# Norm factors on the results of four stages instead of on their inputs, and tile-by-tile refills, in a two-layer trunk

## Chip, cores and metric

The kernel runs on one core of a Trainium2 chip. The metric is the device time of one execution in microseconds; the runs are given with their median.

## What is computed

A trunk of two layers over x of 1024 tokens by 1024 features, in float32. Each layer adds a mixer and a gated feed-forward part, each behind an RMS norm:

```python
def rmsnorm(x, g):
    y = xf * lax.rsqrt(jnp.mean(xf * xf, axis=-1, keepdims=True) + RMS_EPS)
    return y * g
...
for l in range(DEPTH):
    h = rmsnorm(x, norm_mix[l])
    proj = h @ w_in[l]
    (u, dq, dk, dv, iq, ik, iw, rq, rk, rv, rg) = jnp.split(proj, split_pts, axis=-1)
    mix = concatenate([s5(u, ...), sparse_attention(dq, dk, dv, iq, ik, iw, ...), retention(rq, rk, rv, rg, ...)])
    x = x + mix @ w_out[l]
    h = rmsnorm(x, norm_ffn[l])
    gate, up = jnp.split(h @ w_ffn_in[l], 2, axis=-1)
    x = x + (silu(gate) * up) @ w_ffn_out[l]
return rmsnorm(x, norm_final)
```

The norm has two parts: a gain for each feature, and a factor 1/rms for each token. Since the matrix product runs over the features, the factor of a token can be multiplied to the product instead of to the input. The sparse attention scores all earlier tokens with a small indexer, keeps the 256 best by 32 rounds of eight maxima each, and attends to those; S5 is a diagonal state-space model; retention is chunkwise.

## The kernel before

**Tiling.** The 1024 tokens are worked on in two halves h of 512. x is kept feature-major: eight tiles of 128 features by 512 tokens (`xs`), the other half waiting in DRAM. The stages are called by layer and half: proj(l,h) with 18 units, mixout(l,h) with 8, ffn(l,h) with 76 (gate and up units that make a chunk of the hidden layer, then down units that add it to x; four chunks of 4, 6, 6 and 6 tiles). A **unit** is one 128-feature tile of results for 512 tokens. The order of stages is proj(0,0), proj(0,1), mixout(0,0), ffn(0,0), mixout(0,1), proj(1,0), ffn(0,1), proj(1,1), mixout(1,0), ffn(1,0), mixout(1,1), ffn(1,1).

**A unit.** A float32 product is made of three passes over halves of the operands: hi x hi, lo x hi and hi x lo, where hi is the operand rounded and lo the rest. A weight tile comes by DMA on SP's queue (three buffers), ACT copies it to `w_hi` (line 723, `prep`, two buffers), POOL subtracts it to `w_lo` (line 625, three buffers). The input tiles stand in `h_hi` and `h_lo`, eight each, for a whole stage: ACT makes hi (`tile_hi`, line 741), POOL the even lo tiles (line 633) and DVE the odd ones (line 1017, 1065). PE (`unit`, line 1511) takes tile by tile hi, lo and the weight's lo, 24 matmuls of 512 columns. In the first unit after a refill (`fresh`) it does all passes on hi tiles first, each behind its `h_hi_ready`, then those on lo tiles. Results alternate between PSUM banks A and B; retention's units of proj go to four banks, token-major.

**The norm between stages.** `norm()` in the plan is three steps, and a fourth fills the tiles. Squares of x are made by ACT after each x tile's last addition (line 737) and added by POOL into `ssq` (line 642). `sums` (line 1619) multiplies ssq by a column of ones into bank F, `rstd` (lines 833 and 1029) makes the factor for each token, with ACT's square root, `spread` (lines 1039 and 1628) turns it into a diagonal on DVE and spreads it over the partitions of bank F by a matmul, and `fillnorm` (line 1044) multiplies each x tile by gain and factor on DVE (line 1061) for ACT and POOL to split. All tiles wait until the last unit of the stage before is done. `fillmix` does the same for the mixers' outputs, with no norm.

**Evictions.** proj: ACT (lines 751 to 771). mixout and down: DVE adds the bank to x (`add_x`, line 1011). Gate: ACT's Silu from the bank (line 796); up: DVE multiplies the bank by it (line 1103), then ACT and POOL split the product to `a_hi` and `a_lo` (lines 801, 696).

**The order of the work.** `plan()` writes one list of steps, and every engine walks it in order and does its share of each step, so an engine's queue is this list. `weave` spreads the side steps of a stage (top-k rounds, scores, attends, retention, S5) among its units by the estimates of `cost`:

```python
    if step[0] == "attend":
        return 0.3 + 2.2 * NK[step[3]] / 1000 * step[5]
...
    def norm():
        return [("sums",), ("rstd", None), ("spread",)]
...
        got += mix[:1] + list(lead) + weave(mix[1:], side[:n_mix], 0, N_OUT - 2) + norm()
        got += [("fillnorm", "xs", DEPTH + l, ffn[0][-1])] + weave(ffn, side[n_mix:], 0, len(ffn) - 10)
```

A stage's list of units has one step more than it has units: the last one, without matmuls, is the eviction of the last unit (the diff calls it the drain).

## Time and profile before

| | us |
|---|---|
| runs, median of 3 | 2931.11 (2929.31 to 2935.93) |
| the profiled execution | 2937.97 |
| its span in the profile | 2936.2 |
| PE busy in the span | 2643.7 (90%) |
| DVE, POOL, ACT busy | 1519.3, 1264.6, 1011.9 |
| mean granted TensorE clock | 0.94 |

The profile is of one execution, so durations are read against its own time, 2937.97. Of the span, 1.8 us lie around the profile. The chain that ended last runs through PE for 72% of the span and through DVE for 16%. "Busy" is summed over an engine's instructions; an engine that is off the chain may idle without cost.

### The profile page before, as it was taken

What the parts mean: (1) busy time and instruction counts of PE and PEld (TensorE: products, weight loads), DVE (VectorE), ACT (ScalarE), POOL (GpSimd) and SP (SyncE); (2) the same over time, 40 slices, a digit from 0 to 9 for tenths busy, and PEclk for the clock granted to TensorE, in tenths of its full rate; (3) what the DMA queues carried; (4) which work ended last, traced back from release to release, by engine and by line L of the source; (5) the groups of instructions that cost most, each with busy time, mean ns of one, the idle gap of its engine ahead of it and who ended that gap; (6) DMA issues with size and microseconds to landing.
All of it is one profiled execution on the core that took longest, in us unless ns stands there. A gap on an engine that the chain in (4) does not pass through costs nothing.

```text
span 2936.2 us, 34071 instructions
## 1 busy us (share of the span) xinstructions
PE 2643.7 (90%) x13418; PEld 2082.3 (71%) x13418; DVE 1519.3 (52%) x2722; ACT 1011.9 (34%) x1492; POOL 1264.6 (43%) x772
## 2 busy tenths in 40 slices
PE   7877687798999998899999989979899989899998
PEld 5666554577777776668877767757677767678887
DVE  4559822669889522663333146566988962211111
ACT  4222133233444443232343532333344344322222
POOL 3322122344444455354544453344444445555555
PEclk9978886999999999999999999999999999999999
DMA  6321110212222125222322242111222222433332
GB/s 154 89 80 47 30 36 1 72 51 72 74 78 79 58 84 148 77 79 72 88 77 82 58 134 64 54 58 51 71 69 83 72 65 79 143 94 99 113 105 93
DMA packets 389735, 230.24 MB, mean 78 GB/s; under 512 B 33576, under 2 KB 376520, under 8 KB 387528
## 3 DMA queue, kind: packets, MB, share of 16 engines
q1 hardware_dynamic: 388256, 225.44, 26.2%
q10 hardware_dynamic: 1320, 2.62, 0.5%
q8 instruction: 107, 1.75, 0.2%
q14 instruction: 52, 0.43, 0.0%
HBM read 211.78 MB, written 14.16 MB: 77 GB/s over the span
## 4 chain that ended last, share of the span: by engine, by line
PE 72%; DVE 16%; ACT 3%; DMA 3%; POOL 3%; issue 2%; SPq 1%; DVEq 0%; POOLq 0%; ACTq 0%
PE psum L1500 69%; DVE scores L1139 3%; DVE top L1137 3%; PE psum L1781 2%; POOL w_lo L625 1%; DVE tmp L1061 1%; DMA w_raw<-in_w_in_dram 1%; DVE xs L1011 1%; DVE scores L1128 1%; DMA w_raw<-in_w_out_dram 1%; DMA x_half<-xs 1%; POOL h_lo L633 1%; ACT scratch L906 1%; ACT w_hi L723 1%; ACT scratch L888 0%
## 5 line engine op out<-in xcount | busy, mean ns | idle before, releaser
L625 POOL TENSOR_TENSOR w_lo<-w_raw,w_hi 128x1024 fp32r<-128x1024 f32 (+2 forms) x408 | 902.5, 2213 | 1396.2 <-ACT w_hi L723 1377.1
L1500 PE MATMUL psum<-h_hi,w_hi 128*128 128x512 f32 x1984 | 814.9, 411 | 57.3 <-POOL w_lo L625 32.7
L1500 PE MATMUL psum<-h_hi,w_lo 128*128 128x512 f32 x1984 | 793.7, 400 | 0.0
L1500 PE MATMUL psum<-h_lo,w_hi 128*128 128x512 f32 x1984 | 771.4, 396 | 0.0
L723 ACT ACTIVATE w_hi<-w_raw 128x1024 fp32r<-128x1024 f32 (+2 forms) x408 | 396.9, 973 | 893.3 <-PE psum L1500 812.9
L1500 PEld LDWEIGHTS psum<-h_hi,w_hi 128*128 128x128 f32 x1984 | 388.3, 196 | 180.7 <-issue 49.8
L1500 PEld LDWEIGHTS psum<-h_hi,w_lo 128*128 128x128 f32 x1984 | 387.0, 195 | 83.0
L1500 PEld LDWEIGHTS psum<-h_lo,w_hi 128*128 128x128 f32 x1984 | 381.0, 192 | 77.1 <-issue 0.5
L1137 DVE MAX8 top<-scores 128x8 f32<-128x512 f32 (+5 forms) x384 | 342.2, 891 | 8.4
L1139 DVE MATCH_REPLACE8 scores<-top,scores 128x512 f32<-128x512 f32 (+5 forms) x384 | 336.3, 876 | 0.0
L1011 DVE TENSOR_TENSOR xs<-xs,psum 128x512 f32<-128x512 f32 x160 | 110.0, 687 | 358.7 <-PE psum L1500 347.7
L1500 PE MATMUL psum<-a_hi,w_hi 128*128 128x512 f32 x704 | 279.9, 398 | 9.1 <-DVE xs L1011 9.1
L1103 DVE TENSOR_TENSOR tmp<-psum,tmp 128x512 f32<-128x512 f32 x88 | 60.8, 691 | 425.7 <-PE psum L1500 413.4
L1500 PE MATMUL psum<-a_lo,w_hi 128*128 128x512 f32 x704 | 276.6, 393 | 0.8 <-POOL a_lo L696 0.8
L1500 PE MATMUL psum<-a_hi,w_lo 128*128 128x512 f32 x704 | 276.3, 393 | 0.0
L1500 PEld LDWEIGHTS psum<-a_hi,w_hi 128*128 128x128 f32 x704 | 133.4, 189 | 43.3 <-POOL w_lo L625 12.4
L1500 PEld LDWEIGHTS psum<-a_lo,w_hi 128*128 128x128 f32 x704 | 133.4, 190 | 30.8 <-POOL a_lo L696 2.5
L796 ACT ACTIVATE tmp<-psum 128x512 f32<-128x512 f32 x88 | 52.6, 598 | 297.2 <-PE psum L1500 297.0
L1500 PEld LDWEIGHTS psum<-a_hi,w_lo 128*128 128x128 f32 x704 | 133.5, 190 | 26.9
L1170 DVE CUSTOM_DVE_ANT_0 psum<-psum,scores 128x384 f32<-128x384 f32 (+5 forms) x48 | 43.1, 899 | 160.9 <-PE psum L1500 160.2
L1500 PE MATMUL psum<-w_hi,h_hi 128*128 128x512 f32 x256 | 106.4, 416 | 16.9 <-POOL w_lo L625 10.0
L696 POOL TENSOR_TENSOR a_lo<-tmp,a_hi 128x512 fp32r<-128x512 f32 x88 | 119.7, 1360 | 0.0
(262 smaller groups left out, 2906.2 us busy)
## 6 DMA issues: line engine op xcount, KB each, us to landing
w_raw<-in_w_ffn_in_dram SPq DMA_DIRECT2D x176, 512.0 KB, 3.8
w_raw<-in_w_ffn_out_dram SPq DMA_DIRECT2D x96, 384.0 KB, 3.4
w_raw<-in_w_in_dram SPq DMA_DIRECT2D x68, 512.0 KB, 3.7
w_raw<-in_w_out_dram SPq DMA_DIRECT2D x32, 512.0 KB, 4.2
w_raw<-in_w_ffn_out_dram SPq DMA_DIRECT2D x32, 256.0 KB, 2.7
x_half<-xs SPq DMA_DIRECT2D x6, 1024.0 KB, 6.1
xs<-x_half SPq DMA_DIRECT2D x6, 1024.0 KB, 7.1
out_dram<-mixed SPq DMA_DIRECT2D x8, 512.0 KB, 3.7
```

The costliest lines, as they stand in the source:

```text
L625: eng.tensor_tensor(w_lo(u, n), w_raw[:, u % 3, 0:n], w_hi[:, u % 2, 0:n].bitcast(F32), ALU.subtract).then_inc(sems["weights_ready"], 1)
L633: eng.tensor_tensor(h_lo[:, k, :], src, h_hi[:, k, :].bitcast(F32), ALU.subtract).then_inc(sems["h_lo_pool"], 1)
L696: eng.tensor_tensor(a_lo[:, f, :], atmp, a_hi[:, f, :].bitcast(F32), ALU.subtract).then_inc(sems["a_lo_ready"], 1)
L723: act(w_hi[:, u % 2, 0:n], w_raw[:, u % 3, 0:n], ACTF.Copy).then_inc(sems["hi_ready"], 1)
L796: act(gate, bank(unit_bank("ffn", i - 1)), ACTF.Silu).then_inc(sems["gate_ready"], 1)
L1011: tt(xs[:, m, :], xs[:, m, :], bank(g), ADD).then_inc(sems["x_added"], 1)
L1103: tt(atmp, bank(g), gate, MUL).then_inc(sems["atmp_ready"], 1)
L1137: eng.max(out=top8[:, :], in_=score[b]).then_inc(sems["round_step"], 1)
L1139: eng.match_replace(out=score[b], in_to_replace=top8[:, :], in_values=score[b], imm_value=TAKEN).then_inc(sems["round_step"], 1)
L1170: eng.tensor_tensor_reduce(bank(g, 0, nk), bank(g, 0, nk), rows_[r], -1.0, 3e38, ADD, ALU.min, nmax[:, i:i + 1]).then_inc(sems["nmax_ready ...
L1500: return eng.matmul(out_, lhsT, rhs, start=start, stop=stop, skip_group_check=True)
L1781: ins = eng.transpose(bank(g, k * P, (k + 1) * P), at_.prob[:, r, k * P:(k + 1) * P], ident)
```

## The change

In four stages, proj(1,1), ffn(0,0), ffn(1,0) and ffn(1,1) (`deferred`), the input tiles are filled with x times gain, without the token's factor, by ACT (`raw_hi`) and DVE (`raw_lo`) alone, each tile once the last unit of the stage before has read it (`tile_read`), or, for proj(1,1), as each x tile is finished. The sums are made inside the first unit, between its hi and lo passes; the last tile's square goes straight into the sums' matmul instead of through POOL's addition, which makes eight one-column products of the four. The factor, spread over the partitions, is copied to an SBUF tile `row` by ACT, and the results are multiplied by it: in proj(1,1) at eviction, now on DVE (`scale_out`), for retention's token-major units as ACT's scale and DVE's scalar; in ffn the gate by DVE (to `scaled`), then Silu on ACT, then a second multiplication by `row` on POOL, which stands for the up result's factor, then the up multiplication as before.

The other refills (proj(0,1), proj(1,0), ffn(0,1), both `fillmix`) also run tile by tile behind `tile_read` (`tile_free`) and stand ahead of the last eviction in the plan; `fillmix` takes the tiles in an order of its own. The plan moves side steps: attends are costed flatter, retention steps 0 to 3 go from proj(0,0) to proj(0,1), the S5 steps of proj(1,1) end by unit 14, and the factor for ffn(0,1) is made after unit 15 of proj(1,0).

The core of the diff ("..." stands for what is left out):

```diff
-        return 0.3 + 2.2 * NK[step[3]] / 1000 * step[5]
+        return 0.3 + (1.7, 2.2)[step[5]] * NK[step[3]] / 1000
...
+    def scales():
+        return [("rstd", None), ("spread", "row")]
...
-    out += weave(main[15:], [("rstd", "boot"), ("spread",)] + blend(retention_steps(0, 0, 0, 4), rounds(2, 20)))
+    out += main[15:16] + [("rstd", "boot"), ("spread", "fill")] + weave(main[16:18], rounds(2, 20))
+    drain = main[18:]
-    out += [("fillnorm", "xa", 0, main[0][-1]), ("dma", "store_x1_first", main[0][-1]), ("dma", "load_bias", 0)]
+    out += [("fillnorm", "xa", 0, main[0][-1], "tmp")] + drain
+    out += [("dma", "store_x1_first", main[0][-1]), ("dma", "load_bias", 0)]
     s5 = [("s5", 0, s) for s in range(14)]
-    out += weave(main[:14], blend(retention_steps(0, 0, 4) + s5, rounds(3)), 2)
+    out += weave(main[:14], blend(retention_steps(0, 0) + s5, rounds(3)), 0)
...
-        got = [] if h else [("fillmix", l, h, mix[0][-1])]
-        got += mix[:1] + list(lead) + weave(mix[1:], side[:n_mix], 0, N_OUT - 2) + norm()
-        got += [("fillnorm", "xs", DEPTH + l, ffn[0][-1])] + weave(ffn, side[n_mix:], 0, len(ffn) - 10)
+        got = mix[:1] + list(lead) + weave(mix[1:N_OUT], side[:n_mix], 0, N_OUT - 2)
+        got += [("fillraw", DEPTH + l, 0)] + mix[N_OUT:] + [("fillraw", DEPTH + l, 1), ("sums", "inside")]
+        got += ffn[:1] + scales() + weave(ffn[1:], side[n_mix:], 0, len(ffn) - 11)
...
-    out += [("fillnorm", "xa", 1, main[0][-1])]
-    side = [("dma", "s5_load1", 0), ("sums",)]
+    out += [("fillnorm", "xa", 1, main[0][-1], "scratch")] + drain
...
-    out += weave(main[7:], sc[:3] + blend(rounds(2), sc[3:]) + [("spread",)])
+    out += weave(main[7:16], sc[:3] + blend(rounds(2), sc[3:])) + [("spread", "fill")] + main[16:18]
     ffn = window("ffn", 0, 1)
-    out += [("fillnorm", "xs", DEPTH, ffn[0][-1])]
+    out += [("fillnorm", "xs", DEPTH, ffn[0][-1], "tmp")] + main[18:]
...
-    out += norm()
     main = window("proj", 1, 1)
-    out += [("fillnorm", "xs", 1, main[0][-1]), ("dma", "swap_x", main[0][-1])]
-    out += weave(main, [("s5", 1, s) for s in range(14)], 2)
+    out += [("sums", "inside")] + main[:1] + scales() + [("dma", "swap_x", main[0][-1])]
+    out += weave(main[1:N_PROJ], [("s5", 1, s) for s in range(14)], 1, 14)
+    out += [("fillmix", 1, 0, counter[0])] + main[N_PROJ:]
...
+def deferred(kind, l, h):
+    return (kind, l, h) == ("proj", 1, 1) or kind == "ffn" and (l, h) != (0, 1)
+def mix_order(l):
+    return (2, 3, 4, 5, 6, 0, 1, 7) if l else (0, 1, 6, 7, 2, 3, 4, 5)
...
-                    eng.wait_ge(sems["norm_tmp"], st.now("norm_tmp"))
+                    eng.wait_ge(sems["h_lo_dve"], st.now("h_lo_dve"))
...
+                        if did == "gate" and deferred(kind, l, h):
+                            eng.wait_ge(sems["gate_ready"], st.add("gate_ready"))
+                            eng.tensor_tensor(gate, gate, row, ALU.mult).then_inc(sems["gate_scaled"], 1)
...
+            def raw_hi(k, gain):
+                act(h_hi[:, k, :], xs[:, k, :], ACTF.Copy, scale=gains[:, gain, k:k + 1]).then_inc(sems["h_hi_ready"], 1)
+            def tile_free(k, u=None):
+                if k < KT - 1:
+                    eng.wait_ge(sems["tile_read"], st.now("tile_read") + k + 1)
+                elif u is not None:
+                    eng.wait_ge(sems["unit_done"], u)
...
+                if did == "gate" and later:
+                    eng.wait_ge(sems["gated"], st.add("gated"))
+                    if st.now("atmp_ready"):
+                        eng.wait_ge(sems["atmp_ready"], st.now("atmp_ready"))
+                    act(gate, scaled, ACTF.Silu).then_inc(sems["gate_ready"], 1)
...
+                        if (l, h) == (0, 1):
+                            eng.wait_ge(sems["x_added"], st.now("x_added"))
+                            raw_hi(f, 1)
...
+                elif what == "fillraw":
+                    for k in (KT - 1,) if step[2] else range(KT - 1):
+                        tile_free(k)
+                        raw_hi(k, step[1])
...
+            def raw_lo(k, gain):
+                eng.wait_ge(sems["h_hi_ready"], st.add("h_hi_ready"))
+                eng.wait_ge(sems["x_added"], st.now("x_added"))
+                stt(h_lo[:, k, :], xs[:, k, :], gains[:, gain, k:k + 1], h_hi[:, k, :].bitcast(F32), MUL, SUB).then_inc(
+                    sems["h_lo_dve"], 1)
+                st.add("h_lo_dve")
...
+            def scale_out(h, j, u):
+                g = unit_bank("proj", j)
+                cols = slice(h * HALF, (h + 1) * HALF)
+                eng.wait_ge(sems["unit_done"], u)
+                eng.wait_ge(sems["row_ready"], st.now("row_ready"))
...
+                else:
+                    ins = tt(iqT[:, j - U_IQ, :] if j < U_RET else qT[:, j - U_Q, :], bank(g), row, MUL)
+                ins.then_inc(sems["proj_out"], 1)
...
+                if did == "gate" and later:
                     eng.wait_ge(sems["unit_done"], u)
-                    eng.wait_ge(sems["gate_ready"], st.add("gate_ready"))
+                    eng.wait_ge(sems["row_ready"], st.now("row_ready"))
+                    if st.now("gate_ready"):
+                        eng.wait_ge(sems["gate_ready"], st.now("gate_ready"))
+                    tt(scaled, bank(g), row, MUL).then_inc(sems["gated"], 1)
...
-            def unit(g, u, sem):
+            def unit(g, u, sem, last=False):
                 hi, lo = w_hi[:, u % 2, :], w_lo(u)
                 eng.wait_ge(sems["weights_ready"], u + 1)
                 take(g)
                 out_ = bank(g)
                 if fresh[0]:
-                    fresh[0] = False
-                    for k in range(KT):
+                    order, low_by = fresh[0]
+                    fresh[0] = None
+                    for n, k in enumerate(order):
                         eng.wait_ge(sems["h_hi_ready"], st.add("h_hi_ready"))
-                        mm(out_, hi[:, k * P:(k + 1) * P], h_hi[:, k, :], k == 0, False)
+                        mm(out_, hi[:, k * P:(k + 1) * P], h_hi[:, k, :], n == 0, False)
                         mm(out_, lo[:, k * P:(k + 1) * P], h_hi[:, k, :], False, False)
-                    for k in range(KT):
-                        by = ("h_lo_pool", "h_lo_dve")[k % 2]
+                    if inside[0]:
+                        inside[0] = False
+                        sums()
+                    for n, k in enumerate(order):
+                        by = low_by[k % 2]
                         eng.wait_ge(sems[by], st.add(by))
-                        ins = mm(out_, hi[:, k * P:(k + 1) * P], h_lo[:, k, :], False, k == KT - 1)
+                        ins = mm(out_, hi[:, k * P:(k + 1) * P], h_lo[:, k, :], False, n == KT - 1)
                 else:
                     for k in range(KT):
                         w = slice(k * P, (k + 1) * P)
                         mm(out_, hi[:, w], h_hi[:, k, :], k == 0, False)
                         mm(out_, hi[:, w], h_lo[:, k, :], False, False)
                         ins = mm(out_, lo[:, w], h_hi[:, k, :], False, k == KT - 1)
+                        if last and k < KT - 1:
+                            ins.then_inc(sems["tile_read"], 1)
...
-                eng.wait_ge(sems["ssq_added"], st.add("ssq_added", KT - 1))
+                eng.wait_ge(sems["ssq_added"], st.add("ssq_added", KT - 2))
+                eng.wait_ge(sems["square_ready"], st.add("square_ready", KT))
                 take("F")
                 for t in range(TT):
-                    ins = mm(bank("F", t, t + 1), ssq[:, t * P:(t + 1) * P], ones[:, 0:1], True, True)
+                    mm(bank("F", t, t + 1), ssq[:, t * P:(t + 1) * P], ones[:, 0:1], True, False)
+                    ins = mm(bank("F", t, t + 1), atmp[:, t * P:(t + 1) * P], ones[:, 0:1], False, True)
                 ins.then_inc(sems["sums_ready"], 1)
                 leave("F", "mean_ready")
-            def spread():
+            def spread(what):
                 eng.wait_ge(sems["diag_ready"], st.add("diag_ready"))
                 take("F")
-                mm(bank("F"), ones, gate, True, True).then_inc(sems["spread_ready"], 1)
-                leave("F", "norm_tmp", KT)
+                mm(bank("F"), ones, scaled, True, True).then_inc(sems["spread_ready"], 1)
+                if what == "row":
+                    leave("F", "row_ready")
+                else:
+                    leave("F", "norm_tmp", KT)
```

## Rows read from the trace of the kernel before

**Rows 1.** The page's busy time of each engine: us, share of the span, instructions.

```profile
PE 2643.7 (90%) x13418; PEld 2082.3 (71%) x13418; DVE 1519.3 (52%) x2722; ACT 1011.9 (34%) x1492; POOL 1264.6 (43%) x772
```

**Rows 2.** Timeline, two following units of proj(0,1): start us, us, engine line op, out<-in.

```profile
182.75 0.39 PE L1500 MATMUL psum<-h_hi,w_hi 128*128 128x512 f32 x1
...
188.19 0.39 PE L1500 MATMUL psum<-h_hi,w_hi 128*128 128x512 f32 x1
```

**Rows 3.** Timeline, end of ffn(0,1) to proj(1,1); in brackets idle before and releaser.

```profile
1729.85 0.39 PE L1500 MATMUL psum<-a_lo,w_hi 128*128 128x512 f32 x1
...
1731.70 1.26 POOL L642 TENSOR_TENSOR ssq<-ssq,tmp 128x512 f32<-128x512 f32 x1 [0.74 <-ACT tmp L737]
...
1733.02 1.05 PE L1500 MATMUL psum<-cst,ssq 128*128 128x1 f32 x8 [2.78 <-POOL ssq L642]
...
1735.50 2.08 PE L1500 MATMUL psum<-tmp,cst 128*128 128x512 f32 x2 [1.43 <-DVE tmp L1041]
...
1748.82 0.50 PE L1500 MATMUL psum<-h_hi,w_hi 128*128 128x512 f32 x1 [1.31 <-POOL w_lo L625]
```

**Rows 4.** Timeline, TensorE, mixout(0,0)'s last matmul and ffn(0,0)'s second unit.

```profile
579.61 0.39 PE L1500 MATMUL psum<-h_hi,w_lo 128*128 128x512 f32 x1
...
601.23 0.51 PE L1500 MATMUL psum<-h_hi,w_hi 128*128 128x512 f32 x1
```

**Rows 5.** VectorE's lines L1103 and L1391 (ns min/median/max); timeline of the first S5 step.

```profile
L1103 DVE TENSOR_TENSOR tmp<-psum,tmp x88: 681/692/692, 607.5 to 2889.1; 128x512 f32<-128x512 f32 x88
...
L1391 DVE TENSOR_TENSOR scratch<-s5p,s_bb x8: 691/693/2851, 248.8 to 1819.8; 128x512 f32<-128x512 f32 x8
...
1746.46 2.85 DVE L1391 TENSOR_TENSOR scratch<-s5p,s_bb 128x512 f32<-128x512 f32 x1
...
1757.81 0.69 DVE L1397 TENSOR_TENSOR area<-scratch 64x512 f32<-64x512 f32 x1
```

**Rows 6.** Timeline, TensorE, the factor's matmul in mixout(0,1).

```profile
1133.94 1.02 PE L1500 MATMUL psum<-tmp,cst 128*128 128x512 f32 x2
```

**Rows 7.** Gate eviction (page: busy, mean ns, idle) and POOL's low halves (ns min/median/max).

```profile
L796 ACT ACTIVATE tmp<-psum 128x512 f32<-128x512 f32 x88 | 52.6, 598 | 297.2 <-PE psum L1500 297.0
...
L625 POOL TENSOR_TENSOR w_lo<-w_raw,w_hi x408: 1263/2388/3450, 19.6 to 2915.1; 128x1024 fp32r<-128x1024 f32 x96, 128x768 fp32r<-128x768 f32 x28, 128x512 fp32r<-128x512 f32 x12
```

**Rows 8.** Stretches: us, busy of PE, PEld, DVE, ACT, POOL (x), PEclk, DMA share, GB/s.

```profile
176.00:200.00 24.00, 22.67 (x110) 18.51 (x109) 4.96 (x13) 3.54 (x6) 7.67 (x4) 0.93 0.25 67
260.00:300.00 40.00, 35.14 (x268) 27.98 (x266) 38.46 (x96) 7.50 (x10) 7.26 (x3) 0.93 0.14 40
702.00:776.00 74.00, 74.00 (x389) 59.79 (x390) 62.11 (x102) 34.54 (x50) 36.67 (x23) 0.98 0.25 72
776.00:828.00 52.00, 48.87 (x261) 38.35 (x261) 50.33 (x74) 17.10 (x25) 23.68 (x18) 1.00 0.26 74
```

**Rows 9.** Timeline, end of proj(0,0) to the norm for proj(0,1).

```profile
142.90 1.21 DVE L1196 TENSOR_TENSOR scratch<-scratch,cst 128x1024 f32<-128x1024 f32 x1
...
155.22 0.39 PE L1500 MATMUL psum<-h_hi,w_lo 128*128 128x512 f32 x1
...
167.76 2.71 DVE L1061 SCALAR_TENSOR_TENSOR tmp<-area,gains,psum 128x512 f32<-128x512 f32 x4
```

**Rows 10.** Timeline, TensorE: proj(1,0) to ffn(0,1), then the S5 output to mixout(1,0).

```profile
1277.17 0.39 PE L1500 MATMUL psum<-h_hi,w_lo 128*128 128x512 f32 x1
...
1294.51 0.50 PE L1500 MATMUL psum<-h_hi,w_hi 128*128 128x512 f32 x1 [1.30 <-POOL w_lo L625]
...
1890.05 7.03 PE L1500 MATMUL psum<-uy,s_glu 128*128 128x512 f32 x16
...
1910.73 0.50 PE L1500 MATMUL psum<-h_hi,w_hi 128*128 128x512 f32 x1 [1.28 <-POOL w_lo L625]
```

**Rows 11.** Timeline, TensorE, one attend step of block 7 in ffn(0,0).

```profile
1006.84 2.75 PE L1781 MATMUL psum<-cst,scratch 128*128 128x128 f32 x16 [2.62 <-ACT scratch L906]
```

**Rows 12.** The page's group of the top-k rounds' first operation (busy, mean ns, idle).

```profile
L1137 DVE MAX8 top<-scores 128x8 f32<-128x512 f32 (+5 forms) x384 | 342.2, 891 | 8.4
```

More of the change, by code:

```diff
@@ L353, in part @@
             return where[:, first:first + n].rearrange(pattern, **sizes)
-        gate, atmp = tmp[:, 2, :], tmp[:, 3, :]
+        row, scaled, gate, atmp = (tmp[:, i, :] for i in range(4))
         xa = area[:, 0:4096].rearrange("p (k c) -> p k c", k=KT)
@@ L584, in _ @@
                         [383, P], [P * 384, HEADS], [1, 256]])).then_inc(sems["bias_loaded"], 16)
-                elif what == "fillnorm":
-                    st.add("norm_tmp", KT)
+                elif what in ("fillnorm", "fillmix"):
+                    st.add("h_lo_dve", KT // 2)
+                elif what == "fillraw" and step[2]:
+                    st.add("h_lo_dve", KT)
                 elif step[:2] == ("dma", "store_x1_first"):
@@ L791, in ffn @@
                 did, c, f = FFN[i - 1] if i else (None, 0, 0)
-                if did == "gate":
+                later = deferred("ffn", l, h)
+                if did == "gate" and not later:
                     eng.wait_ge(sems["unit_done"], u)
@@ L1874, in _ @@
                 elif what == "sums":
-                    sums()
+                    if step[1] == "inside":
+                        inside[0] = True
+                    else:
+                        sums()
                 elif what == "rstd":
```

171 lines of the change are left out of this document (125 added, 46 removed).

## The prediction

> **What bounds the kernel now.** I began with the busy time of each engine over the span: TensorE (PE) is busy 90% of it, VectorE (DVE) 52%, GpSimd (POOL) 43%, ScalarE (ACT) 34% [rows 1]. So a gain must come from PE's idle 10%, or from work that PE itself needn't do. Next I read the timeline at the ends of the stages, since there each engine works for the next and PE can only wait. The measure is a unit: inside a stage, the first matmuls of two following units stand 5.44 us apart [rows 2], which is 24 matmuls of 0.227. Where a stage hands over, I take the end of its last unit (start of the last matmul plus 0.23) and the start of the second unit of the next stage; what that distance has above 5.44 is lost.
>
> Between ffn(0,1) and proj(1,1) the last matmul starts at 1729.85 and the second unit at 1748.82 [rows 3]: 18.74 us, **13.3 lost**. The rows between show why: POOL's last addition of squares (1.26), the sums on PE (1.05), 1.43 until the factor's matmul, then that matmul (2.08), and only then are the eight input tiles normed, copied and split. mixout(1,1) to ffn(1,1) repeats it to 0.1. mixout(0,0) to ffn(0,0) has 601.23 - 579.84 = 21.4 [rows 4]; without the unit and eight score matmuls (8 x 0.227 = 1.8) it is 14.1, and mixout(1,0) to ffn(1,0) repeats it. The four add up to 54.8.
>
> **The change, part by part**
>
> *Norm factors on the results, four stages.* The tiles need no factor now, so ACT and DVE refill each as the last unit leaves it. Tile 7 comes last: addition 0.69 (a DVE operation of this size [rows 5]), then a square and a copy on ACT; PE's 16 hi matmuls of the first unit take 3.6 us, so the tile is there before its turn. What stays on PE's path is the sums, doubled (the last square now enters by matmuls of its own, 2 x 1.05 = 2.1), and the factor's matmul, 1.02 where the clock is up [rows 6], against 2.08 in the junction now. The factor needs 1.43 after the sums and eight lo matmuls (1.8) cover that. The second unit's weights (ACT copy, then POOL 2.39 [rows 7]) are ready near 5.7 us after the junction's start, PE needs them at 7.5. So about 3.1 stays at each of four junctions, 12.4 in all: **+42.4**. With the factor's matmul at its low-clock price it would be 38.2.
>
> *The gate's new path.* In 66 gates of three ffn stages the eviction was one ACT operation (0.60 [rows 7]) and is now DVE 0.69, ACT 0.60, POOL 1.26 (the size of POOL's addition [rows 3]), then DVE as before. PE waits for none of it directly: the bank is free after the first. POOL does the next weights first (ACT copy about 1, POOL 2.39, to 3.4 after the unit's end) and its multiplication ends near 5.0, before the up unit ends at 5.44, when DVE needs it. I take **0**. The cover is the idle of these engines: in a stretch of ffn(0,0) with about two top-k rounds to a unit DVE is busy 62.11 of 74 us and POOL 36.67 [rows 8], and per pair of units (10.9 us) the change adds 0.69 and 1.26. Where DVE has no idle (776 to 828: 50.33 of 52 [rows 8]) mostly downs run, which have no gate.
>
> A DVE operation with two inputs in SBUF took 2.85 us instead of 0.69 while POOL worked [rows 5], and the up multiplication, which reads one input from PSUM, took 0.68 to 0.69 in all 88 cases [rows 5]. The Trainium skill, "SBUF — State Buffer", section "SBUF: two separate sides", says that a VectorE operation with two SBUF inputs and a GpSimd operation that reads SBUF hold one port pair in turn, each for its whole length; this speaks against the change, since its new POOL multiplications read SBUF. By that rule every one could hold DVE up to 1.26 us; by the rows half or more of the eight such operations weren't held at all (median 0.69 [rows 5]). My sum goes by the rows, and the other price is in the first rival.
>
> *proj(0,0) to proj(0,1).* Last unit's end 155.45, then eight DVE operations of the retention kind (one of 1.21 has its row) run ahead of the norm's DVE work, which starts at 167.76 [rows 9]. The change moves these retention steps into proj(0,1), so 8 x 1.21 = 9.7 us leave the path. There they meet DVE idle 19 of 24 us at the stage's start, but DVE busy 38.46 of 40 later on [rows 8]. Bounds: 0, if the later stretch pays it all back, and 19, if that idle takes all that was waited for. I take the nearest row: **+10**.
>
> *The other refills.* proj(1,0) to ffn(0,1): 1294.51 - 1277.40 = 17.1 [rows 10], 11.7 lost. The factor is now ready before the last unit ends and the tiles are filled while it runs; the matmul for the factor (1.02) and about 1 of DVE wait stay: **+9.5**. mixout(0,1) to proj(1,0) gets the same treatment, but ACT's last square and the second unit's weights stand behind the refill, bounds 0 and 9.5; I take **+1**, since its factor is on the chip well before the end already (its matmul is the one of [rows 6]), so only the refill itself gets earlier. mixout(1,0)'s inputs: PE ends the S5 output at 1897.08 (1890.05 + 7.03) and the second unit starts at 1910.73 [rows 10], 8.2 lost; filling five tiles ahead of the S5 tiles hides it: **+8**. The same in layer 0, where the attention's tiles come last and are only there when the attention is: bounds 0 and 8.2, near the low one, **+1.5**.
>
> *Side steps.* In proj(1,1) the S5 steps are squeezed from units 2 to 18 into 2 to 14, and all evictions move from ACT to DVE, behind them. The first S5 step holds DVE from 1746.46 to 1758.5, 12.0 us [rows 5]; one unit of cover leaves 6.6: **-7** (without the slow operations it is about 4.3 shorter, so -2; twice, -13). The last attends of ffn(0,0) and ffn(1,0) now come nearly one to a unit. Back to back, PE waits 2.62 before one [rows 11], some 3 with the step after it; two such pairs less per stage, two stages: **+12** (0 if the waits only move). In exchange the downs of chunk 2 get 16 rounds instead of 14: two rounds of two operations of 0.89 [rows 12] are 3.6 us on a DVE without idle, **-6** for two stages with a little taken off. The DMAs that swap x in proj(1,1) stand one unit later on SP's queue and wait for the eight low tiles; weight loads queue behind them, but run up to three units ahead (16 us), and that wait ends by the first unit's end: 0.
>
> *Sums elsewhere.* Three more sums double (3 x 1.05): **-3**. At the very end POOL's 1.26 goes and 1.05 comes: **+0.2**.
>
> **Sum:** 42.4 + 10 + 9.5 + 1 + 8 + 1.5 - 7 + 12 - 6 - 3 + 0.2 = 68.6. The profiled execution took 2937.97 us (span 2936.2); so it would take 2869.4. The median of the runs is 6.9 below that execution, so the prediction is **2862**. The three runs lie 0.23% apart, so 0.2% (6 us) is about what can be told from no change.
>
> **Rivals**
>
> *VectorE gives part back.* The proj(0,1) gain is eaten by the stage's own DVE-bound stretch (-10), S5 stalls PE twice (-6 more), the attends' waits only move (-12), and POOL's multiplications hold DVE as in the 2.85 case [rows 5]: the 74 us [rows 8] hold seven pairs, 7 x (0.69 + 1.26) = 13.7 against 11.9 us of idle, 1.8 over, and some three such stretches lie in the two stages (-6, rounded up). This leaves 34.6: **2896**. For it: DVE 38.46 of 40 [rows 8]. Against: the first three items need a stretch without idle, and DVE has idle in most. By the rule of the Trainium skill ("SBUF — State Buffer", as above) the last item is the likely one.
>
> *More comes free.* proj(0,1) takes its full 19 (+9), S5 costs only 2 (+5), the extra rounds lie in idle (+6): **2842**.
>
> *The gate's path becomes the bound, and the kernel slower.* POOL works in order: if DVE takes up a gate's result late, because a round or an S5 or attend piece is ahead of it, ACT's Silu and POOL's multiplication wait, and behind that POOL's next weights wait, for which PE waits. It decides once the multiplication ends over 3 us later than 5.0. At 2 us in each of 44 gates with side work, 88 us: 2950. At 1.5 to 1.7 it only cancels the gain. For it: three engines in a row instead of one; against: 3 us of slack, and DVE's free time [rows 8].
>
> *Deferring does nothing.* If tile 7, or the sums inside the first unit, hold the second unit as long as the normed fill does now, 42.4 go: 2905. The junction's rows speak against it [rows 3], as nearly all of the 13.3 lies in steps that the tiles don't need any more.
>
> **How the numbers follow.** Forecast 0.62 (own range 2850 to 2875), VectorE gives back 0.15, more free 0.10, deferral without effect 0.03, gate path 0.10 (0.07 slower, 0.03 no change). The range 2838 to 2896 holds the first three, with a little more at the low end for the low-end terms together. Faster 0.90, same 0.03, slower 0.07.
>
> **What would show it.** Right: at the four junctions the second unit starts some 8.5 us after the last unit's end (10.4 with the scores); the factor's matmul after the first unit takes about 1; a gate's POOL multiplication ends before its up unit; PE's wait for POOL's weights doesn't grow in ffn(0,0). Wrong in part: PE idle before DVE operations early in proj(1,1), or proj(0,1) as long as before by its end. Wrong altogether: PE idle before w_lo in most gates, with POOL waiting for ACT's Silu.

## The result and the profile after

The changed kernel took **2907.41 us** (median of 4 runs, 2898.05 to 2907.97) against 2932.86 before (median of 4 runs); the ratio is 0.9903, 95% interval 0.989 to 0.9916. It is faster by 1.0%. Forecast were 2862 us and 2838 to 2896, so the sign is right, and the gain is 25 us of the 69 that were summed up.

The page of the changed kernel, the busy time of its engines [rows 1] and the shares of the chain that ended last:

```profile
span 2905.5 us, 34447 instructions
PE 2638.2 (91%) x13482; PEld 2082.5 (72%) x13482; DVE 1558.2 (54%) x2784; ACT 1013.9 (35%) x1484; POOL 1313.1 (45%) x814
...
PE 70%; DVE 18%; issue 3%; ACT 3%; POOL 3%; DMA 2%; SPq 0%; DVEq 0%; ACTq 0%; POOLq 0%
```

PE is busy 5.5 us less, although it has 64 more one-column matmuls to do; the share of the chain that ended last on VectorE rose from 16% to 18%. To see where the time went I cut the execution at the ends of the stages (start of a stage's last matmul plus 0.23) and set the lengths beside the forecast's terms (us):

| from the end of the stage before to the end of | before | after | gain | forecast |
|---|---|---|---|---|
| proj(0,0) | 155.5 | 155.5 | 0.0 | 0 |
| proj(0,1) | 280.3 | 280.2 | 0.1 | 10 |
| mixout(0,0) | 144.1 | 140.9 | 3.2 | 1.5 |
| ffn(0,0) | 516.9 | 512.1 | 4.8 | 14 |
| mixout(0,1), proj(1,0), ffn(0,1) | 633.4 | 634.0 | -0.7 | 8.4 |
| proj(1,1), mixout(1,0) | 246.6 | 237.7 | 9.0 | 11.2 |
| ffn(1,0) | 515.6 | 510.6 | 5.1 | 14 |
| mixout(1,1), ffn(1,1), the end | 443.8 | 434.6 | 9.3 | 9.4 |

The sum is 30.7, the difference of the two profiled spans. (14 is deferring 11, attends 6, rounds -3; the 11.2 and 9.4 are sums of the prediction's terms in the same way.) Three places miss: proj(0,1) by 10, the group with proj(1,0) by 9, ffn(0,0) and ffn(1,0) by 9 each. The rest is within 2.2, though two of the rows agree only as sums: proj(1,1) grew by 2.5 and mixout(1,0) shrank by 11.5 (forecast were 3.2 and 8 less), since S5 steps that ran behind proj(1,1) now run in it.

The junctions themselves came out nearly as forecast. Timeline of PE at the end of ffn(0,1) [rows 3] (the columns are those of [rows 2]):

```profile
1722.48 0.39 PE L1638 MATMUL psum<-a_lo,w_hi 128*128 128x512 f32 x1
1722.70 0.39 PE L1638 MATMUL psum<-h_hi,w_hi 128*128 128x512 f32 x1
...
1726.33 0.28 PE L1638 MATMUL psum<-cst,ssq 128*128 128x1 f32 x2
...
1728.03 2.11 PE L1638 MATMUL psum<-h_lo,w_hi 128*128 128x512 f32 x8
1729.98 1.02 PE L1638 MATMUL psum<-tmp,cst 128*128 128x512 f32 x2
1730.44 0.79 PE L1638 MATMUL psum<-h_hi,w_hi 128*128 128x512 f32 x1
```

The first unit follows the last without a gap, the sums take 1.70 (to 1728.03), the factor 0.46, and the second unit starts 7.73 after the end of the stage: 2.3 lost where it was 13.3, and 3.1 forecast. At ffn(0,0) the same 7.73. But two units on in ffn(0,0) [rows 4]:

```profile
576.56 0.39 PE L1638 MATMUL psum<-h_hi,w_hi 128*128 128x512 f32 x1
...
584.29 0.79 PE L1638 MATMUL psum<-h_hi,w_hi 128*128 128x512 f32 x1
...
592.08 1.99 PE L1638 MATMUL psum<-ikT,iqT 64*128 64x512 f32 x8 [1.74 <-DVE scores L1257]
...
605.54 2.82 PE L1959 MATMUL psum<-cst,scratch 128*128 128x128 f32 x12 [5.79 <-DVE scratch L1332]
```

PE waits 1.74 us for the score step's VectorE operation and 5.79 for the retention step's. Before, the scores' wait (2.0) lay in the time that the junction lost anyway, and PE waited 0.33 for the retention's operation. In all, PE's waits from the end of mixout(0,0) to the end of unit 20 of ffn(0,0) (counted from 0) come to 16.5 us before and 16.4 after: the junction's time became waits for the side steps.

proj(0,1) shows the swap most plainly. The matmul that stood behind the normed fill [rows 9] waited 11.67 in the kernel before:

```profile
174.41 0.79 PE L1500 MATMUL psum<-mixed 64*128 64x128 f32 x2 [11.67 <-DVE tmp L1061]
```

and in the kernel after the tiles cost 4.18, and the next wait is 11.74 for the retention steps that were moved here:

```profile
158.20 2.72 DVE L1151 SCALAR_TENSOR_TENSOR tmp<-area,gains,psum 128x512 f32<-128x512 f32 x4
...
159.81 0.77 PE L1638 MATMUL psum<-h_hi,w_hi 128*128 128x512 f32 x1 [4.18 <-ACT h_hi L777]
...
167.05 6.70 POOL L646 TENSOR_TENSOR w_lo<-w_raw,w_hi 128x1024 fp32r<-128x1024 f32 x2 [0.48 <-ACT w_hi L753]
...
168.18 3.36 DVE L1326 TENSOR_TENSOR scratch<-scratch,cst 128x1024 f32<-128x1024 f32 x1
...
179.93 1.33 PE L1959 MATMUL psum<-cst,scratch 128*128 128x128 f32 x5 [11.74 <-DVE scratch L1332]
...
1157.13 0.50 PE L1638 MATMUL psum<-h_hi,w_hi 128*128 128x512 f32 x1 [3.64 <-POOL w_lo L646]
...
1209.72 1.50 PE L1638 MATMUL psum<-ikT,iqT 64*128 64x384 f32 x4 [2.03 <-DVE scores L1257]
1213.19 2.08 PE L1638 MATMUL psum<-ikT,iqT 64*128 64x512 f32 x4 [1.97 <-DVE scores L1257]
...
1265.64 1.12 PE L1638 MATMUL psum<-tmp,cst 128*128 128x512 f32 x2 [1.39 <-DVE tmp L1123]
```

The fill does start 9.6 us earlier (158.20 against 167.76), as the forecast's 9.7 has it. But the moved steps now stand behind it on VectorE, up to 179.9, and one of their operations took 3.36 us instead of 1.21, while POOL made the weights' low halves. The last four lines are of proj(1,0): the second unit waits 3.64 for its weights (1.32 before), PE waits twice about 2.0 for scores (once before), and 1.39 for the factor's diagonal in the middle of the stage.

### The profile page after: what moved, and what is told of

It is laid out like the page before. It is cut to its first block, busy times and chain, and to the rows that moved or that the text cites. A ratio compares the mean times of both kernels' runs of the same rounds, so it can differ in the third digit from the quotient of the medians.

```text
span 2905.5 us, 34447 instructions
## 1 busy us (share of the span) xinstructions
PE 2638.2 (91%) x13482; PEld 2082.5 (72%) x13482; DVE 1558.2 (54%) x2784; ACT 1013.9 (35%) x1484; POOL 1313.1 (45%) x814
## 4 chain that ended last, share of the span: by engine, by line
PE 70%; DVE 18%; issue 3%; ACT 3%; POOL 3%; DMA 2%; SPq 0%; DVEq 0%; ACTq 0%; POOLq 0%
PE psum L1638 66%; DVE scores L1268 4%; DVE top L1266 4%; PE psum L1933 2%; POOL w_lo L646 2%; DMA w_raw<-in_w_in_dram 1%; DVE scores L1257 1%; DVE xs L1093 1%; DMA w_raw<-in_w_out_dram 1%; ACT scratch L971 1%; ACT w_hi L753 1%; POOL h_lo L654 1%; DVE psum L1299 0%; PE psum L1819 0%; DMA x_half<-xs 0%
## 5 line engine op out<-in xcount | busy, mean ns | idle before, releaser
L1230 DVE TENSOR_TENSOR tmp<-psum,tmp 128x512 f32<-128x512 f32 x88 | 60.8, 691 | 280.7 <-PE psum L1638 279.5
L1219 DVE TENSOR_TENSOR tmp<-psum,tmp 128x512 f32<-128x512 f32 x66 | 45.5, 690 | 130.0 <-PE psum L1638 121.5
```

Source lines behind the costliest of these rows:

```text
L1219: tt(scaled, bank(g), row, MUL).then_inc(sems["gated"], 1)
L1230: tt(atmp, bank(g), gate, MUL).then_inc(sems["atmp_ready"], 1)
```

## The experiments

Of each run the stage lengths below are taken as in the table above, from its profile; a stage that no edit touches still scatters from run to run: proj(0,0) from 153.5 to 157.2, proj(0,1) of the changed kernel from 277.1 to 280.3, proj(1,0) from 132.6 to 136.0, ffn(0,1) from 440.4 to 445.2 and ffn(1,1) from 368.7 to 370.4, but ffn(0,0) only from 511.6 to 512.2 and ffn(1,0) from 510.6 to 512.3. The scatter goes with TensorE's mean granted clock: proj(1,0) took 136.0 at 0.92 and 132.6 at 0.96, ffn(0,1) 445.2 at 0.98 and 440.4 at 0.99, and the changed kernel's four runs 2907 to 2908 at 0.945 to 0.947 and 2898.05 at 0.950. So medians less than about 10 us apart say little by themselves; the stages that an edit touches say more.

### Is it VectorE's throughput? Half of the rounds, in both kernels

```diff
-    return [("round", b, r) for r in range(first, last)]
+    return [("round", b, r) for r in range(first, last) if r % 2]
```

> The kernel before with every second top-k round left out in all blocks (16 of 32, so that another set of tokens is attended to), in the same places of the plan. It is the base for the next run and tells little alone. If VectorE's rounds set the pace of proj(0,1), proj(1,0) and the ffn stages of half 0, it is 60 us or more faster than the kernel before; if PE sets it, within 20 us.

> The changed kernel with the same rounds left out. Theory (VectorE's work sets the length of the stages in which the junctions' gain was lost): without half of the rounds the gain stays, so ffn(0,0) and ffn(1,0), from the end of the stage before to their own end, are 11 us or more shorter than in the base run (they were 4.8 and 5.1 shorter with all rounds), proj(1,0) is no more than 2 us longer (was 7.5 longer), and the pair lies 45 us or more apart (was 31). Rival (the gates' longer path costs PE something in each gate, whatever the rounds): ffn(0,0) and ffn(1,0) stay about 5 shorter and the pair about 31 apart.

Measured: 2860.3 and 2820.65 us, 39.7 apart (47.1 in the profiled spans), between the two expectations. proj(1,0) was only 2.4 longer (7.5 with all rounds). ffn(0,0) became 8.2 shorter, ffn(1,0) 4.1, proj(0,1) 1.1. So the theory holds nearly for proj(1,0) (2.4 for 2), half for ffn(0,0) (8.2 for 11), and fails for ffn(1,0) and proj(0,1): with half of the rounds gone the junction's time is lost there all the same. The amount of VectorE's work carries a part of the loss (the pair lies 14 us further apart than with all rounds), not all of it. The plan places side steps by their cost, so with fewer rounds they also stand in other units; the pair doesn't separate the two.

### Is it the gate's longer path?

```diff
-                    eng.wait_ge(sems["gated"], st.add("gated"))
+                    eng.wait_ge(sems["unit_done"], u)
...
-                    act(gate, scaled, ACTF.Silu).then_inc(sems["gate_ready"], 1)
+                    act(gate, bank(unit_bank("ffn", i - 1)), ACTF.Silu).then_inc(sems["gate_ready"], 1)
...
```

> The changed kernel with the gates evicted as before, by ACT's Silu straight from PSUM; the token factor inside Silu is left out, POOL's multiplication stays. Theory: VectorE gets 22 x 0.69 us back in each of the deferred ffn stages; where it sets the pace (about the first 13 units of ffn(0,0) and ffn(1,0)) this shortens the stage: 5 to 9 us less in each of the two, within 1.5 us in ffn(1,1), in all 10 to 18 us less than the changed kernel. Rival (the loss is from the side steps standing one unit later, or from POOL): under 3 us each.

```diff
-                            eng.tensor_tensor(gate, gate, row, ALU.mult).then_inc(sems["gate_scaled"], 1)
```

> The changed kernel without POOL's multiplication of the gate by the factor (the up result's factor is left out). Theory (VectorE's own work is what counts): within 2 us in ffn(0,0), ffn(1,0) and ffn(1,1) each. Rival (POOL's multiplication holds VectorE at the SBUF port or delays POOL's weights): 4 to 13 us less in ffn(0,0) and ffn(1,0) each, and VectorE's max and match-replace operations are shorter in the mean there.

Measured: 2899.09 and 2900.97 us. With plain gates ffn(0,0) was 2.5 shorter, ffn(1,0) 0.7 longer, ffn(1,1) 1.8 shorter; without POOL's multiplication 0.0, 1.7 longer and 1.8 shorter. The medians are 8.3 and 6.4 below the changed kernel's, but of the profiled spans' 7.9 and 5.2 only 3.6 and 0.1 lie in the three stages that the edits touch; the rest is scatter elsewhere, and so is the 1.8 in ffn(1,1) (368.7 in runs that leave it as it is). The first run's theory (5 to 9 us from each of two stages) falls, with 2.5 from one; of the second run the theory stands and the rival falls: neither the 66 VectorE operations nor POOL's hold up much. Taking the gate's path at 0 was right within 4 us. By line, the changed kernel's operations (ns min/median/max):

```profile
L1219 DVE TENSOR_TENSOR tmp<-psum,tmp x66: 677/692/693, 585.6 to 2851.8; 128x512 f32<-128x512 f32 x66
...
L717 POOL TENSOR_TENSOR tmp<-tmp x66: 1268/1294/1491, 588.9 to 2854.5; 128x512 f32<-128x512 f32 x66
```

### Do the side steps stand in the wrong place?

With the gate's path gone and the rounds explaining only a part, what was left was where the plan puts the side steps. First the units of before, behind the scales:

```diff
-        return 0.3 + (1.7, 2.2)[step[5]] * NK[step[3]] / 1000
+        return 0.3 + 2.2 * NK[step[3]] / 1000 * step[5]
...
-        got += ffn[:1] + scales() + weave(ffn[1:], side[n_mix:], 0, len(ffn) - 11)
+        woven = weave(ffn, side[n_mix:], 0, len(ffn) - 10)
+        got += woven[:1] + scales() + woven[1:]
```

> The changed kernel with the side steps of ffn(0,0) and ffn(1,0) in the units in which they stood before (from unit 0 on, behind the scales, and with the old cost of attends). New theory, since gates and rounds explained too little: the junction's gain is lost where the plan now lets PE run into a retention step (PE waited 5.8 us for its VectorE operation in unit 2, 3.3 in unit 13), as the side steps start one unit later and are woven tighter. Then that wait goes from 5.8 to under 2 and the two ffn stages are 4 to 8 us shorter each, less what the attends of block 7 lose again (2 to 4). Rival (VectorE's total work sets the pace, wherever the steps stand): the wait shows up elsewhere, and each stage is within 2 us of the changed kernel.

Measured (run side_old): 2916.34 us, ffn(0,0) 4.5 and ffn(1,0) 8.1 longer than in the changed kernel. PE's waits in ffn(0,0):

```profile
588.80 3.42 PE L1639 MATMUL psum<-ikT,iqT 64*128 64x512 f32 x8 [4.33 <-DVE scores L1258]
...
604.83 1.97 PE L1960 MATMUL psum<-cst,scratch 128*128 128x128 f32 x16 [1.50 <-DVE scratch L1333]
...
671.59 0.47 PE L1639 MATMUL psum<-a_hi,w_hi 128*128 128x512 f32 x1 [3.02 <-DVE xs L1094]
678.59 0.76 PE L1639 MATMUL psum<-a_hi,w_hi 128*128 128x512 f32 x1 [3.99 <-DVE xs L1094]
...
697.90 0.80 PE L1639 MATMUL psum<-h_hi,w_hi 128*128 128x512 f32 x1 [2.52 <-POOL w_lo L647]
```

The 5.79 is 1.50 now, but the scores' wait is 4.33 instead of 1.74, and the later ones are longer too: up to unit 20 PE's waits for VectorE and POOL come to 15.9 with the old places and 15.7 with the new. The rival is right here as far as the wait goes: it moves. On the stages' lengths it is wrong (it said within 2), and so is the theory, which had them shorter. The length comes mostly from the attends: their old cost is dearer at the end of the side work: units 57 to 66 take 3.7 us longer in ffn(0,0) and 7.2 in ffn(1,0), so the flatter attends bring about the 6 per stage that they were given.

Then further apart instead of earlier:

```diff
+    if step[0] in ("scores", "retention") and step[2] == 1 and step[3] >= (7 if step[0] == "scores" else 2):
+        return 4.5
```

> The changed kernel with the last score steps and the retention steps of ffn(0,0) and ffn(1,0) set further apart (their estimate in the plan 4.5 instead of 2 and 3), so that a unit more lies between two of them; the attends of block 7 get denser for it (3, 3 and 2 to a unit). Theory: after the faster junction PE stands at the next link of a chain (scores: PE, ACT, VectorE; retention: VectorE, PE) before the link ahead is done, and what the junction gave is waited away there; with a unit between, PE's waits for retention's VectorE operations (5.8 and 3.3 us) and scores (1.7) fall to under 4 in all, 5 us or more less up to the end of unit 16, of which the attends take back 2 to 5. Rival (the sum of the work on VectorE sets the pace there): the waits for VectorE up to unit 20 stay above 9 us in all.

Measured (run space): 2917.57 us. The waits for scores and retention up to unit 20 fell from 10.8 to 5.2 (5.79 to 1.51, the other retention wait 3.27 to 1.94), but ffn(0,0) is 10.3 longer, ffn(1,0) 5.9: PE's waits for ACT in the denser attends after unit 20 rose from 12.6 to 23.3. Apart, the links do seem to cover each other, nearly as the theory says (5.2 for under 4); but the edit also moves seven of 34 top-k rounds and two of three attends out of the first 20 units, so less is asked of VectorE there, and that work has to be done later: it costs more at the other end.

### What deferring is worth in ffn(0,0) and ffn(1,0)

```diff
-    return (kind, l, h) == ("proj", 1, 1) or kind == "ffn" and (l, h) != (0, 1)
+    return (kind, l, h) == ("proj", 1, 1) or kind == "ffn" and (l, h) == (1, 1)
...
+        if h == 0:
+            got = mix[:1] + list(lead) + weave(mix[1:], side[:n_mix], 0, N_OUT - 2)
+            got += [("sums", None), ("rstd", None), ("spread", "fill"), ("fillnorm", "xs", DEPTH + l, ffn[0][-1], "tmp")]
+            return got + ffn[:1] + weave(ffn[1:], side[n_mix:], 0, len(ffn) - 11)
```

> The changed kernel with the normed fill back in ffn(0,0) and ffn(1,0) (sums, factor and fill between the stages, plain gates), all side steps where the change puts them. Theory: of the 13.3 us that deferring takes out of the junction, little is left at the stage's end, so these two stages are no more than 6 us longer each than in the changed kernel, and PE's waits for scores and retention in units 1 to 3 fall, since the junction covers them. Rival (as I predicted: the junction's time comes straight off the end, and something else in the stage costs it): 10 us or more longer each.

Measured (run norm_ffn0): 2914.27 us; ffn(0,0) is 6.7 longer than in the changed kernel and ffn(1,0) 5.3, one just above the theory's 6 and one below. The second unit ends 10.3 us later. By unit 20 the lead of the deferred fill is 9.6 in ffn(0,0) and 11.2 in ffn(1,0); then it melts, 1.8 where the downs with many rounds begin (unit 30), 1.0 in two places after that, 3.0 at block 7's attends in ffn(1,0) alone. One thing speaks against the theory: the retention wait is the same with the normed fill.

```profile
580.48 2.08 PE L1642 MATMUL psum<-tmp,cst 128*128 128x512 f32 x2 [1.43 <-DVE tmp L1127]
...
593.80 0.50 PE L1642 MATMUL psum<-h_hi,w_hi 128*128 128x512 f32 x1 [1.23 <-POOL w_lo L650]
...
612.92 1.33 PE L1963 MATMUL psum<-cst,scratch 128*128 128x128 f32 x5 [5.82 <-DVE scratch L1336]
```

So that wait belongs to the new places of the steps, not to the faster junction. The four kernels side by side, from the end of mixout(0,0) to the end of unit 20 of ffn(0,0):

| us | side steps of before | side steps of the change |
|---|---|---|
| normed fill | 149.1 (before) | 157.5 (norm_ffn0) |
| deferred | 148.9 (side_old) | 147.8 (the change) |

The new places have one top-k round more done by then. With the old places the first unit ends 10.0 us earlier (7.3 instead of 17.3 after the stage before), and by unit 20 **0.2** of it is left; with the new places deferring gives 9.6, but the new places alone cost 8.3. Together 1.3 is left by unit 20.

The whole stages, ffn(0,0) and ffn(1,0), tell it differently:

| us | side steps of before | side steps of the change |
|---|---|---|
| normed fill | 516.9, 515.6 | 518.8, 515.9 |
| deferred | 516.6, 518.7 | 512.1, 510.6 |

Most of the 8.3 comes back at the attends of units 57 to 66, which are 6 us shorter with the new places. By the end the new places alone cost 1.9 and about 0.2, and deferring alone gives 0.3 and loses 3.1; only the two together gain, 4.8 and 5.1.

### proj(0,1): one wait for another

```diff
-    out += main[15:16] + [("rstd", "boot"), ("spread", "fill")] + weave(main[16:18], rounds(2, 20))
+    out += main[15:16] + [("rstd", "boot"), ("spread", "fill"), ("retention", 0, 0, 0)]
+    out += weave(main[16:18], blend(retention_steps(0, 0, 1, 3), rounds(2, 20)))
...
+    out += [("retention", 0, 0, 3)]
...
-    out += weave(main[:14], blend(retention_steps(0, 0) + s5, rounds(3)), 0)
+    out += weave(main[:14], blend(retention_steps(0, 0, 4) + s5, rounds(3)), 2)
```

> The changed kernel with retention steps 0 to 3 back in proj(0,0). Theory: in proj(0,1) one wait took the place of another (PE waited 11.7 us for the normed tiles before, now 11.7 for the retention's VectorE operation), because both stand in VectorE's queue one behind the other. Then with the steps back PE waits again about 8 to 12 us for the tiles, the 11.7 at the retention falls to under 3, and the stage is as long as now within 4 us. Rival (the tile-by-tile refill alone brings the gain, and the moved steps cost it): the stage is 8 us or more shorter.

```diff
-    out += weave(main[:14], blend(retention_steps(0, 0) + s5, rounds(3)), 0)
+    out += weave(main[:6], blend(retention_steps(0, 0), rounds(3, 0, 12)), 2)
+    out += weave(main[6:14], blend(s5, rounds(3, 12)))
```

> The changed kernel with all 14 retention steps of proj(0,1) in units 2 to 5 instead of 0 to 5, and S5 from unit 6. Theory as in the run before: what lacks is cover on PE while VectorE works off the refill and the first retention steps, so with three units ahead of them (16 us) the 11.7 us wait falls to under 3 and the stage is 5 us or more shorter. Rival (the chain of retention and S5 steps between VectorE, ACT and PE sets the stage's length): the wait moves to later steps, and the stage is within 4 us of now.

Measured (runs ret_back and ret_from2): 2908.93 us with the steps back, the stage 283.9 (280.2 in the changed kernel). The waits are again at the early retention steps, 4.18 and then 13.69 ahead of the matmul that waited 11.67 before:

```profile
159.95 3.68 PE L1961 MATMUL psum<-cst,scratch 128*128 128x128 f32 x16 [4.18 <-DVE scratch L1334]
...
176.19 1.03 ACT L993 ACTIVATE mixed<-psum 128x1024 f32<-128x1024 f32 x1
...
177.31 1.24 PE L1640 MATMUL psum<-mixed 64*128 64x128 f32 x8 [13.69 <-issue]
```

The profile names no releaser for the 13.69, but ACT's copy to `mixed` ends at 177.22, just before that matmul; it stands behind the refill's copies on ACT. So the theory holds in the main: moving steps across the boundary moves the wait. The edit is not quite the old order: step 3 stands behind the refill here, ahead of it in the kernel before. mixout(0,0), too, took 144.8 in that run, near the 144.1 of the kernel before, against 140.9 in the changed kernel, at a granted clock of 0.76 against 0.81. Over both stages the moved steps are thus worth 7.6; with the refill but without them the two stages are 4.3 longer than in the kernel before. How much of that is the clock is not shown. With more units ahead of them (ret_from2, 2901.22 us) the 11.74 falls to 0.47, but the stage is 277.0, no shorter than the unchanged one of norm_ffn0 (277.1): later waits, at retention's end (12.42) and between S5 steps, take it. The second theory falls to its rival, as the wait moves on. That the chain of links between PE, ACT and VectorE alone sets the length of proj(0,1) is not shown: with half of the rounds the stage is 17 to 18 us shorter in either kernel (263.5 and 262.4), so VectorE's load counts there as well.

### proj(1,0): rounds squeezed ahead of the factor

```diff
-    out += weave(main[7:16], sc[:3] + blend(rounds(2), sc[3:])) + [("spread", "fill")] + main[16:18]
+    woven = weave(main[7:18], sc[:3] + blend(rounds(2, 0, 24), sc[3:]))
+    at = woven.index(main[16])
+    out += woven[:at] + [("spread", "fill")] + woven[at:]
...
-    side = blend(retention_steps(1, 0), rounds(3, 0, 16)) + attend_steps(1, 0, 0)
+    side = rounds(2, 24) + blend(retention_steps(1, 0), rounds(3, 0, 16)) + attend_steps(1, 0, 0)
```

> The changed kernel with the top-k rounds of block 2 spread over units 7 to 17 of proj(1,0), the last eight of 32 in the first units of ffn(0,1), and the factor's matmul still after unit 15. Theory: proj(1,0) grew by 7.5 us as 32 rounds and the score steps were squeezed into nine units (PE's waits for scores rose from 2.0 to 5.1, and it waited 1.4 for the factor's diagonal); relaxed, proj(1,0) is 3 to 5 us shorter and ffn(0,1) no more than 1 longer. Rival (the growth is from the doubled sums and from the second unit's weights, 3.6 us at w_lo): under 2 shorter.

Measured (run proj10_later): **2891.73 us**, ratio to the kernel before 0.9862 (0.9846 to 0.9879), against 0.9903 (0.989 to 0.9916) of the change. proj(1,0) is 126.5, 7.2 shorter than in the changed kernel, which is more than the theory said, and ffn(0,1), at 440.3, took over the last eight rounds for nothing (it has 440.4 untouched in two other runs). The untouched proj(1,0) scatters from 132.6 to 136.0; at the same granted clock of 0.96 it is 132.6, so 6.1 of the 7.2 don't come from the clock. Of the 20 us between the two profiled executions the other 13 lie in stages that the edit leaves alone, or in ffn(0,1), which is as short in runs without it. The two extra waits are gone; what is left of the three in the changed kernel is one for scores, beside the second unit's weights:

```profile
1155.84 0.50 PE L1640 MATMUL psum<-h_hi,w_hi 128*128 128x512 f32 x1 [3.62 <-POOL w_lo L648]
...
1209.12 0.92 PE L1640 MATMUL psum<-ikT,iqT 64*128 64x384 f32 x4 [2.03 <-DVE scores L1259]
```

### Together

> The changed kernel with the rounds of block 2 spread as in proj10_later and the retention steps of proj(0,1) as in ret_from2. If the two gains are of different stages, they add up: proj(0,1) about 277, proj(1,0) and ffn(0,1) together 12 us less than the changed kernel, the median 2885 to 2890. If they were partly chance from run to run, the median is nearer to 2900.

The second adds to this:

```diff
-    out += [("fillnorm", "xa", 1, main[0][-1], "scratch")] + drain
+    out += [("fillnorm", "xa", 1, main[0][-1], "scratch")] + main[:1] + drain
```

> As combo1, and at the start of proj(1,0) ACT copies the second unit's weights ahead of the last square. Theory: the refill gains little there since the second unit then waits 3.6 us for its weights, which stand behind the refill and the square on ACT; with the square behind them this wait falls by 1 to 2 us. Rival (POOL's own low tiles hold them): no change within 0.5.

Measured (runs combo1 and combo2): 2891.47 and 2890.24 us (0.9867 and 0.9863, with intervals that hold both and proj10_later). The expected 2885 to 2890 was just missed: proj(1,0) and ffn(0,1) together are 8.9 and 14.2 shorter than in the changed kernel, around the 12 expected, but ret_from2's edit adds nothing: proj(0,1) was 277.5 and 279.9 in these two. The weights' wait did fall:

```profile
1154.00 0.50 PE L1641 MATMUL psum<-h_hi,w_hi 128*128 128x512 f32 x1 [1.30 <-POOL w_lo L649]
```

It was 3.66 in combo1 and is 1.30 here, a little more than the theory's 1 to 2 less, and proj(1,0) is 122.9 instead of 127.2 (at a granted clock of 0.97 instead of 0.95). The medians of all three lie about 16 us below the changed kernel's; 7.2, 6.5 and 10.8 of that are seen in proj(1,0), the rest is not tied to an edit.

## Why the prediction was wrong

**Right.** The junctions: forecast 3.1 left at each, measured 2.3 at three and 5.0 at ffn(1,1), where PE waits 1.1 for the last tile, which the forecast had there in time, and the granted clock is 0.77 from that wait to the second unit. The gain up to the second units is 54.8 - 11.9 = 42.9, forecast 42.4; that it agrees so closely is partly luck, as the deviations cancel. It stayed where no side chain follows: mixout(1,1) to the end gained 9.3 of 9.4 (in parts 2.6, 7.8 and -1.2). The gate's path at 0: right within 4 us, shown by two runs. The refill of mixout(1,0): with proj(1,1) 9.0 of 11.2. The attends: 3.7 and 7.2, forecast 6. mixout(0,0) gained 3.2 where 1.5 was forecast for its refill, but it gained nothing in ret_back, which has that refill; so this gain is not shown to be the refill's.

**Wrong step 1: a junction's time counted as the stage's.** "42.4" was taken whole from the end of the kernel. In ffn(0,0) and ffn(1,0) the side steps follow at once, as a chain (PE's scores, ACT, VectorE, PE's retention, VectorE), and before the change part of that chain ran while PE stood at the junction. I saw the score matmuls there and took out only their 1.8 us of work, not the wait in front of them. The tables of four kernels show the rest: deferring alone gives 0.2 by unit 20 of ffn(0,0), and at the stages' ends 0.3 and -3.1; with the new places of the side steps it gives 6.7 and 5.3, where 11 was forecast. Which link sets the pace in the first 20 units is still open: half of the rounds and plain gates did not free it.

**Wrong step 2: the moved side steps of ffn(0,0) and ffn(1,0) counted by their attends alone.** That they start a unit later and are woven tighter stands in the diff, and I priced only block 7 and chunk 2. With the normed fill their new places cost 8.3 us up to unit 20; the attends later return 6 of that, and at the stages' ends 1.9 and 0.2 are lost, where a gain of 3 each was forecast (6 for the attends less 3 for the rounds).

**Wrong step 3: proj(0,1), +10.** I bounded it with 0 at the low end, and VectorE's idle 19 of 24 us at the stage's start made me take the "nearest row". But that idle was time in which VectorE had nothing to do yet, not room: PE needs the moved steps' results at once, and waited 11.74 for them. Measured 0.1; the first rival had this item, though as a loss in the later stretch.

**Wrong step 4: proj(1,0) to ffn(0,1), +9.5, with "about 1 of DVE wait".** The refill brought most of what it should (the second unit of ffn(0,1) starts 9.55 after the end of proj(1,0), 17.1 before, 7.6 gained of 9.5). But to have the factor ready, 32 rounds and the scores were squeezed into nine units. That cost proj(1,0) 7.5 us, and proj10_later gives back 7.2.

**The rivals.** "VectorE gives part back" was the right one by kind, at 2896; its item for proj(0,1) held in direction, its second S5 stall did not come (PE waits 5.60 once for the first S5 step of proj(1,1), where the forecast itself had 6.6), the attends' waits did not only move, its item on POOL's multiplications did not happen (without them ffn(0,0) is as long and ffn(1,0) no shorter), and it had neither ffn(0,0)'s first units nor proj(1,0). By the rule of the Trainium skill ("SBUF — State Buffer", "SBUF: two separate sides") the 66 new POOL operations could hold VectorE; no run here shows that these cost time. POOL's making of the weights' low halves, which the kernel before has too, did hold one in proj(0,1): the 3.36 us above lie in the chain that PE waited for. "The gate's path becomes the bound" and "deferring does nothing" are refuted as they were put. The second has the nearest number, 2905, but by luck: the second units do start 7.73 us after the stage's end, and the gain is spent behind them. The range was too narrow because all that it held shared the junction's 42.4.

## What to carry to other kernels

A gap on the busiest engine is worth its length only if nothing that follows was being made ready in it: before counting it, list the next cross-engine results that this engine will ask for, and when each could be there without the gap. A side step that is moved must be priced at its new place, by the wait of its first consumer, not by its busy time. Where a stage's length is a chain over several engines, moving links earlier, later or apart moved the wait in four trials here; taking work out of one crowded stretch (proj(1,0), 7.2 us) was what paid.

## What the runs showed of the hardware that I had not expected

Short matmuls cost PE less than their listed duration: sixteen one-column records in place of eight took 1.70 us from first start to the next matmul, where I had doubled 1.05; the factor's two matmuls are listed at 1.02 us, but the next one starts 0.46 later. On PE the price is the distance between starts.

A VectorE operation with one input in PSUM was not held while POOL worked: of the 66 above, 18 ran during a POOL operation, and all took 677 to 693 ns. The one with two SBUF inputs that fills the low tiles was, each time:

```profile
L1130 DVE SCALAR_TENSOR_TENSOR h_lo<-xs,gains,h_hi x32: 737/748/2377, 572.7 to 2524.4; 128x512 fp32r<-128x512 f32 x32
```

Of these 32, the 21 that met no POOL operation took 737 to 753 ns, the 11 that met one 1753 to 2377. That agrees with the rule of the Trainium skill named above. Most of the 11 lie at the end of ffn(0,1), where PE has other work; the held operation of proj(0,1) (3.36 us instead of 1.21) lies on PE's path.
